# A four-layer transformer: norm weights on x instead of the matrices, and head probabilities turned by DMA in all layers

## The chip, the cores and the metric

The kernel runs on one core of a Trainium2 chip. A core has TensorE (PE), VectorE (DVE), ScalarE (ACT), GpSimd (POOL) and SyncE (SP), each with its own queue of instructions that it works off in order, and 16 DMA engines. The metric is the time of one execution in microseconds; lower is better.

## The reference, cut to what matters

256 tokens of width 1024 go through four layers. Each layer is attention, a gated feed-forward part (hidden width 2816) and a gate on a side input, each behind a norm:

```python
def rmsnorm(x, g, eps=NORM_EPS):
    xf = x.astype(jnp.float32)
    y = xf * lax.rsqrt(jnp.mean(xf * xf, axis=-1, keepdims=True) + eps)
    return (y * g.astype(jnp.float32)).astype(x.dtype)
...
    for i in range(DEPTH):                       # DEPTH = 2, twice
        hn = rmsnorm(h, norm_mix[i])
        ...                                      # mix = attention(hn): another kind in each of the four layers
        h = h + mix
        h = h + swiglu(rmsnorm(h, norm_ffn[i]), ffn_w_gate[i], ffn_w_up[i], ffn_w_down[i])
        gate = jax.nn.sigmoid(rmsnorm(h, norm_ple[i]) @ ple_w_gate[i])
        h = h + gate * (p[i] @ ple_w_proj[i])
```

The four attentions are differential attention (`L_DA`: `a[0] - lam * a[1]`, then a norm over each head), neighbourhood attention (`L_NA`), stick-breaking attention (`L_SB`) and forgetting attention (`L_FX`: queries and keys have norms of their own, `rms_norm(split_heads(...), ...)`, and its queries see `attn_norm_g`, its keys and values `shared_norm_g`). All are float32.

## The kernel before

**Tiling.** The weights stream through a ring of six slots (`raw`, `RING`) in units of 128 x 1024 floats. A layer is a row of 108 units, numbered `s`: 24 for queries, keys and values (`U_QKV`), 8 for the attention's output (`U_WO`), 4 + 60 for gate and up and down (`U_GU0`, `U_FFN`), 4 for the last down and the side input, 8 for the gate (`U_GATE`). The 16 heads are worked in four groups `j` (0 to 3), each with four query/key units and two value units, so a group takes six units.

**Float32 by three products.** TensorE multiplies in a rounded format. Each factor is split: ACT copies `raw` to the rounded `whi` and DVE takes the rest, `wlo = raw - whi` (`split`); PE then adds three products of each pair (`three`, lines 1618 to 1620; 1729 to 1731 where x stands on the streaming side), 12 products with 512 columns for most units. x is split in the same way into `xhi` and `xlo`. Norm weights multiply the matrix in this step: for units behind a norm, `split` gets a column of `gain` as scale, in two pieces of 512 (`unit_parts`). The norm's root factor is applied behind the products.

**The turned x.** At each norm PE turns h in four quarters (`turn_x`, quarter `q` = half of the columns, half of the rows), into two PSUM banks `tb` in turns; for each quarter ACT writes `xhi` (line 861) and DVE `xlo` (1160), each in one instruction of 128 x 512. At a layer's end DVE computes h quarter by quarter (`gated_side`, 1184 and 1186), with `xlo` of quarters 0 and 1 between; PE turns quarters 2 and 3 in `first_pair`, between its 12 products for the first tile and those for the second.

**Attention.** What runs at which unit is a table for each engine (`PE_STEPS`, `ACT_STEPS`, `DVE_STEPS`): row `r` of group `j` runs at unit `s = 6 j + r + 4`; a name with `+` behind the unit's own work. Per group: scores on PE, bias and maximum on DVE, exponentials on ACT (`exp0`, `exp1` for the two tiles of 128 queries), normalization on DVE (`post0`, `post1`), then the probabilities `z` are turned and multiplied with the values (`pvt`; `pv0`, `pv1`, `turno` in the first layer). `V_WAITS` says at which row the product with the values runs in groups that do not use the table's own.

**Two ways of turning.** PE turns `z` with `turn` (line 1779) in batches of four blocks (`turnp0`, `turnp1`), and ACT (960, 963) and DVE (1389) copy the batches out of PSUM. With `by_dma` true (groups 0 to 2 of the second and third layers), DVE splits each probability into its two 16-bit halves (`split_p`, 1255), SP issues a DMA transpose (554), and ACT joins the halves again (`join`, 946).

**The fourth layer.** ACT squares the raw queries and keys, DVE sums the squares (1340), POOL takes the root (704, 706), DVE scales (1363), and only then can PE turn them (`turnqk0`, `turnqk1`) and compute scores.

## Time and profile before

| | us |
|---|---|
| median of 3 runs (1313.96 to 1315.85) | 1314.66 |
| the profiled execution | 1316.3 |
| its span, first to last instruction | 1314.5 |
| PE busy | 1300.8 |
| DVE busy | 958.0 |
| ACT busy | 847.8 |
| POOL busy | 130.7 |

Read it so: PE has something in flight for 99% of the span, and is TensorE at its upper clock nearly throughout. Matmuls overlap, so the time that one costs is the distance to the next one's start, and a stall is a longer distance. Rows of a timeline carry their own start times, so who is late by how much can be read off.

### The profile page before, as it was taken

The page shows a single profiled execution, that of the slowest core. Times are in us where ns is not written, and L with a number is a line of the kernel's source. Part 1 is how long each engine was busy: PE and PEld are TensorE (multiplying, and loading weights), DVE is VectorE, ACT ScalarE, POOL GpSimd, SP SyncE. Part 2 cuts the span into 40 slices and gives each one's busy share as a digit, 9 for nine tenths or more (in the row PEclk, how much of TensorE's full clock was granted, in tenths as well). Part 3 has the DMA queues.
Part 4 walks back from the last instruction along what each step waited for, and adds up shares of the span by engine and source line. Part 5 has one row for each costly group of instructions (what it writes and reads, how often), then busy time and mean ns, then how long its engine had stood idle before and what let it go on. Part 6 is the DMA issues. An engine that isn't in the chain of part 4 may idle for free.

```text
span 1314.5 us, 20037 instructions
## 1 busy us (share of the span) xinstructions
PE 1300.8 (99%) x6642; PEld 1084.5 (83%) x6642; DVE 958.0 (73%) x1661; ACT 847.8 (64%) x1459; POOL 130.7 (10%) x179
## 2 busy tenths in 40 slices
PE   8999999999999999999999999999999999999998
PEld 7988888888887788888888888888887778888887
DVE  6887687666898766666699976666677887666664
ACT  7666666656777666665676666666578766666654
POOL 6031234410000000000010000000002210000000
PEclk9999999999999999999999999999999999999999
DMA  9444788876496566667647656666655535676671
GB/s 336 145 156 137 221 243 245 239 226 200 167 222 174 162 198 207 207 207 211 210 149 196 181 174 195 210 210 206 212 161 185 178 127 168 199 209 210 209 226 48
DMA packets 205056, 255.28 MB, mean 194 GB/s; under 512 B 72962, under 2 KB 163249, under 8 KB 204992
## 3 DMA queue, kind: packets, MB, share of 16 engines
q1 hardware_dynamic: 201984, 245.42, 60.8%
q0 software_dynamic: 2832, 8.49, 2.8%
q8 instruction: 37, 0.61, 0.2%
q10 hardware_dynamic: 176, 0.54, 0.1%
q14 instruction: 27, 0.22, 0.1%
HBM read 238.33 MB, written 1.13 MB: 182 GB/s over the span
## 4 chain that ended last, share of the span: by engine, by line
PE 92%; DVE 5%; ACT 1%; DMA 1%; issue 1%; SPq 1%; POOL 0%; DVEq 0%; ACTq 0%
PE acc L1618 14%; PE acc L1620 14%; PE acc L1619 14%; PE sc L1620 12%; PE sc L1619 12%; PE sc L1618 12%; PE turn L1779 3%; PE acc L1729 2%; PE acc L1730 2%; PE acc L1731 2%; PE turn L1881 1%; DVE wlo L1140 1%; DMA raw<-in_da_w_qkv 1%; PE sc L1832 1%; DVE z L1299 1%
## 5 line engine op out<-in xcount | busy, mean ns | idle before, releaser
L830 ACT ACTIVATE whi<-raw,aT_gain 128x512 fp32r<-128x512 f32 (+2 forms) x612 | 403.6, 719 | 79.1 <-PE sc L1620 53.4
L1140 DVE SCALAR_TENSOR_TENSOR wlo<-raw,aT_gain,whi 128x512 fp32r<-128x512 f32 (+2 forms) x612 | 431.0, 759 | 28.7 <-ACT whi L830 24.6
L1618 PE MATMUL sc<-whi,xhi 128*128 128x512 f32 x640 | 249.3, 390 | 0.0
L1620 PE MATMUL sc<-whi,xlo 128*128 128x512 f32 x640 | 249.0, 389 | 0.0
L1619 PE MATMUL sc<-wlo,xhi 128*128 128x512 f32 x640 | 249.0, 389 | 0.0
L1618 PE MATMUL acc<-whi,xhi 128*128 128x512 f32 x432 | 173.3, 401 | 1.8 <-DVE wlo L1140 1.4
L1620 PE MATMUL acc<-whi,xlo 128*128 128x512 f32 x432 | 168.5, 390 | 0.0
L1619 PE MATMUL acc<-wlo,xhi 128*128 128x512 f32 x432 | 168.5, 390 | 0.0
L830 ACT ACTIVATE whi<-raw 128x1024 fp32r<-128x1024 f32 x120 | 125.8, 1055 | 63.5 <-PE acc L1620 56.9
L1138 DVE TENSOR_TENSOR wlo<-raw,whi 128x1024 fp32r<-128x1024 f32 x120 | 145.5, 1244 | 0.0
L1619 PEld LDWEIGHTS sc<-wlo,xhi 128*128 128x128 f32 x640 | 120.1, 188 | 25.0
L1618 PEld LDWEIGHTS sc<-whi,xhi 128*128 128x128 f32 x640 | 120.1, 188 | 24.9
L1620 PEld LDWEIGHTS sc<-whi,xlo 128*128 128x128 f32 x640 | 120.1, 188 | 24.7
L1415 DVE SCALAR_TENSOR_TENSOR aT_gain<-sc,rstd,aT_gain 128x256 f32<-128x256 f32 x80 | 38.7, 484 | 114.7 <-ACT aT_gain L979 114.7
L979 ACT ACTIVATE aT_gain<-sc,rstd 128x256 f32<-128x256 f32 x80 | 38.0, 475 | 127.0 <-PE sc L1620 127.0
L1618 PE MATMUL acc<-whi,split_qg 128*128 128x512 f32 x288 | 112.4, 390 | 0.0
L1620 PE MATMUL acc<-whi,split_qg 128*128 128x512 f32 x288 | 112.1, 389 | 0.0
L1619 PE MATMUL acc<-wlo,split_qg 128*128 128x512 f32 x288 | 112.1, 389 | 0.0
L1618 PEld LDWEIGHTS acc<-whi,xhi 128*128 128x128 f32 x432 | 81.3, 188 | 19.0 <-DVE wlo L1140 1.9
L1620 PEld LDWEIGHTS acc<-whi,xlo 128*128 128x128 f32 x432 | 81.1, 188 | 17.4
L673 POOL TENSOR_SCALAR rstd<-ss 128x2 f32<-128x2 f32 x12 | 2.7, 222 | 917.3 <-ACT spare L853 917.3
L1619 PEld LDWEIGHTS acc<-wlo,xhi 128*128 128x128 f32 x432 | 81.4, 189 | 15.0
(213 smaller groups left out, 2069.6 us busy)
## 6 DMA issues: line engine op xcount, KB each, us to landing
raw<-in_ffn_w_gu SPq DMA_DIRECT2D x176, 256.0 KB
raw<-in_qk SPq DMA_DIRECT2D x62, 512.0 KB
raw<-in_ffn_w_gate SPq DMA_DIRECT2D x88, 256.0 KB
raw<-in_ffn_w_up SPq DMA_DIRECT2D x88, 256.0 KB
raw<-in_ffn_w_down SPq DMA_DIRECT2D x44, 512.0 KB
raw<-in_ffn_w_d SPq DMA_DIRECT2D x44, 512.0 KB
raw<-in_ple_w_gate SPq DMA_DIRECT2D x32, 512.0 KB
raw<-in_da_w_qkv SPq DMA_DIRECT2D x8, 512.0 KB
```

Source lines behind the costliest of these rows:

```text
L830: ins = act.activation(whi[:, u % RING, c0:c1], raw[:, u % RING, c0:c1], ACT.Copy, scale=scale)
L979: act.activation(aT[:, 0, t * 256:t * 256 + 256], bank[:, 0:256], ACT.Sigmoid, scale=rs(L, 1, t))\
L1138: ins = dve.tensor_tensor(lo, w, hi.bitcast(F32), ALU.subtract)
L1140: ins = dve.scalar_tensor_tensor(out=lo, in0=w, scalar=gain[:, g:g + 1], in1=hi.bitcast(F32), op0=ALU.mult, op1=ALU.subtract)
L1415: dve.scalar_tensor_tensor(out=sg, in0=banks[t][:, 256:512], scalar=rs(L, 1, t), in1=sg, op0=ALU.mult, op1=ALU.mult).then_inc(gmid, 1)
L1618: pe.matmul(dst, xh, wh, start=first, stop=False)
L1619: pe.matmul(dst, xh, wl, start=False, stop=False)
L1620: return pe.matmul(dst, xl, wh, start=False, stop=last)
L1729: pe.matmul(dst, wh, xh, start=first and k == 0 and c == 0, stop=False)
L1730: pe.matmul(dst, wl, xh, start=False, stop=False)
L1731: ins = pe.matmul(dst, wh, xl, start=False, stop=last and k == 1 and c == 1)
L1779: ins = pe.transpose(tb[e % 2][0:cols, n * rows:(n + 1) * rows], src, ident[0:rows, 0:rows])
```

## The change

1. Norm weights are taken off the matrices. A weight unit behind a norm is now split in one piece of 1024 without scale; the weight columns go onto x where it is split. Since a norm weight belongs to one block of 128 columns of h, each quarter of x is now written in four pieces of 128 x 128 by ACT and four by DVE. DVE begins when ACT's four are done (`turn_hi` counts once a quarter). PE waits for single pieces (`wait_x`) in `first_pair` and at the gate. The fourth layer's first norm keeps its weights on the matrix (two norms share that x), but its x too is written in pieces. The 256 x 1024 input x in the beginning is split in pieces of one block as well.
2. `by_dma` is true for head groups 0 to 2 of all four layers. In the first layer there are two maps to turn and not four (`p_maps`), since the difference is taken ahead.
3. The products with the values move to later rows: in the fourth layer from row 8 to 10, in the first layer for group 1 from rows 6, 7 and 8 to 8, 9 and 10. `join0` and `join1` are added to ACT's tables of both layers.

```diff
@@ tables @@
-    L_DA: [["evacqk"], ["turnqk"], [], ["exp0"], ["exp1"], ["turnp0"], ["pv0", "turnp1"], ["pv1*"], ["turno*"]],
+    L_DA: [["evacqk"], ["turnqk"], [], ["exp0"], ["exp1"], ["turnp0"], ["pv0", "turnp1"], ["pv1*", "join0"],
+           ["turno*", "join1"]],
...
-    L_FX: [["evacqk"], [], ["turnqk0", "turnqk1+"], [], ["exp0", "exp1+"], ["turnp0"], ["turnp1"], ["pvt*"]],
+    L_FX: [["evacqk"], [], ["turnqk0", "turnqk1+"], [], ["exp0", "exp1+"], ["turnp0"], ["turnp1"], ["pvt*"], ["join0"], ["join1"]],
...
-V_WAITS = {L_DA: {"pv0": 8, "pv1": 9, "turno": 10}, L_NA: {"pvt": 9}, L_SB: {"pvt": 10}, L_FX: {"pvt": 8}}
+V_WAITS = {L_DA: {"pv0": 8, "pv1": 9, "turno": 10}, L_NA: {"pvt": 9}, L_SB: {"pvt": 10}, L_FX: {"pvt": 10}}
...
-            if j % 2 == 0 or (L == L_FX or joined(L)) and j < HG - 1:
+            if j < HG - 1:
...
-    return L in (L_NA, L_SB,) and j < HG - 1
+    return L in (L_DA, L_NA, L_SB, L_FX,) and j < HG - 1
@@ ACT, turn_x @@
                     act.wait_ge(turned, e + 1)
-                    act.activation(xhi[:, 4 * hf:4 * hf + 4, t * P:(t + 1) * P],
-                                   tb[e % 2][:, :].rearrange("p (k c) -> p k c", k=4), ACT.Copy).then_inc(turn_hi, 1)
+                    for k in range(4):
+                        g = x_gain(L, n, 4 * hf + k)
+                        ins = act.activation(xhi[:, 4 * hf + k, t * P:(t + 1) * P], tb[e % 2][:, k * P:(k + 1) * P],
+                                             ACT.Copy, scale=1.0 if g is None else gain[:, g:g + 1])
+                    ins.then_inc(turn_hi, 1)
@@ DVE, turn_x @@
+                    dve.wait_ge(turn_hi, SPLIT[("x", L, n, q)])
+                    for k in range(4):
+                        g, at = x_gain(L, n, 4 * hf + k), (slice(None), 4 * hf + k, slice(t * P, (t + 1) * P))
+                        src = tb[e % 2][:, k * P:(k + 1) * P]
...
+                        ins.then_inc(x_lo if k < 3 else turn_out[e % 2], 1)
@@ DVE, after_exp, first layer @@
                     ins.then_inc(a_ready, 1)
+                    if by_dma(L, j):
+                        dve.wait_ge(a_ready, 2 * j + t + 1)
+                        split_p(L, j, t)
                     return
@@ PE, first_pair @@
                         for k in range(2):
+                            wait_x(pe, L, n, t, 2 * b + k)
```

**Order on ACT, fourth layer.** Around the exponentials of group 1 (`z,sums<-z,mx`; `whi` is a weight unit in pieces). Before:

```order
L830 ACTIVATE whi<-raw,aT_gain 128x512 [waits unit_done,weights_in5]
L830 ACTIVATE whi<-raw,aT_gain 128x512
L974 ACTIVATE ohi<-turn 128x512 [waits turned]
L936 ACTIVATE z,sums<-z,mx 128x128 [waits mx_ready]
L936 ACTIVATE z,sums<-z,mx 128x128 x3
L830 ACTIVATE whi<-raw,aT_gain 128x256 [waits unit_done,weights_in0]
L830 ACTIVATE whi<-raw,aT_gain 128x256 x3
L936 ACTIVATE z,sums<-z,mx 128x256 [waits mx_ready]
L936 ACTIVATE z,sums<-z,mx 128x256 x3
L960 ACTIVATE aT_gain<-turn 128x4x128 [waits turned]
L830 ACTIVATE whi<-raw,aT_gain 128x256 [waits unit_done,weights_in1]
```

Now:

```order
L959 ACTIVATE bias<-aT_gain 128x4x128 [waits p_turned0]
L959 ACTIVATE bias<-aT_gain 128x4x128
L841 ACTIVATE whi<-raw,aT_gain 128x512 [waits unit_done,weights_in5]
L841 ACTIVATE whi<-raw,aT_gain 128x512
L949 ACTIVATE z,sums<-z,mx 128x128 [waits mx_ready]
L949 ACTIVATE z,sums<-z,mx 128x128 x3
L959 ACTIVATE bias<-aT_gain 128x1024 [waits p_turned1]
L959 ACTIVATE bias<-aT_gain 128x1024
L841 ACTIVATE whi<-raw,aT_gain 128x256 [waits unit_done,weights_in0]
L841 ACTIVATE whi<-raw,aT_gain 128x256 x3
L949 ACTIVATE z,sums<-z,mx 128x256 [waits mx_ready]
L949 ACTIVATE z,sums<-z,mx 128x256 x3
```

The join of group 0's second tile (`bias<-aT_gain`, 128x1024 twice) stands between the two tiles' exponentials, and the copy of the head output (`ohi`) has moved behind them.

**Order on DVE, fourth layer.** From the normalization of group 0's second tile (`z<-z,rsum`) to the scaling of group 1's queries and keys (`qkv<-acc,r_h`). Before:

```order
L1297 RECIPROCAL rsum<-sums 128x4 [waits e_ready]
L1299 TENSOR_TENSOR z<-z,rsum 128x1024 [waits dve_link]
L1340 TENSOR_REDUCE ss_h<-nab 128x8 [waits sq_ready] x2
L1140 SCALAR_TENSOR_TENSOR wlo<-raw,aT_gain,whi 128x256 [waits hi_done]
L1140 SCALAR_TENSOR_TENSOR wlo<-raw,aT_gain,whi 128x256 x3
L1363 TENSOR_TENSOR qkv<-acc,r_h 128x512 [waits rh_ready] x2
L1389 COPY aT_gain<-turn 128x512 [waits turned]
```

Now:

```order
L1321 RECIPROCAL rsum<-sums 128x4 [waits e_ready]
L1323 TENSOR_TENSOR z<-z,rsum 128x1024 [waits dve_link]
L1276 COPY bias<-z 128x1024 [waits p_ready]
L1276 COPY bias<-z 128x1024
L1364 TENSOR_REDUCE ss_h<-nab 128x8 [waits sq_ready] x2
L1156 SCALAR_TENSOR_TENSOR wlo<-raw,aT_gain,whi 128x256 [waits hi_done]
L1156 SCALAR_TENSOR_TENSOR wlo<-raw,aT_gain,whi 128x256 x3
L1387 TENSOR_TENSOR qkv<-acc,r_h 128x512 [waits rh_ready] x2
```

Two copies (`bias<-z`) stand ahead of the sum of squares (`ss_h<-nab`), and the copy of turned probabilities (`aT_gain<-turn`) is gone.

**Order on DVE, end of the first layer.** Quarters 1 to 3 of h and of `xlo`. Before:

```order
L1184 TENSOR_TENSOR aT_gain<-aT_gain,z 128x512 [waits proj_out,gate_sig]
L1186 TENSOR_TENSOR h<-h,aT_gain 128x512 [waits gated]
L1160 TENSOR_TENSOR xlo<-turn,xhi 128x4x128 [waits turn_hi]
L1184 TENSOR_TENSOR aT_gain<-aT_gain,z 128x512 [waits proj_out,gate_sig]
L1186 TENSOR_TENSOR h<-h,aT_gain 128x512 [waits gated]
L1160 TENSOR_TENSOR xlo<-turn,xhi 128x4x128 [waits turn_hi]
L1184 TENSOR_TENSOR aT_gain<-aT_gain,z 128x512 [waits proj_out,gate_sig]
L1186 TENSOR_TENSOR h<-h,aT_gain 128x512 [waits gated]
```

Now:

```order
L1205 TENSOR_TENSOR aT_gain<-aT_gain,z 128x512 [waits proj_out,gate_sig]
L1207 TENSOR_TENSOR h<-h,aT_gain 128x512 [waits gated]
L1187 SCALAR_TENSOR_TENSOR xlo<-turn,aT_gain,xhi 128x128 [waits turn_hi]
L1187 SCALAR_TENSOR_TENSOR xlo<-turn,aT_gain,xhi 128x128 x3
L1205 TENSOR_TENSOR aT_gain<-aT_gain,z 128x512 [waits proj_out,gate_sig]
L1207 TENSOR_TENSOR h<-h,aT_gain 128x512 [waits gated]
L1187 SCALAR_TENSOR_TENSOR xlo<-turn,aT_gain,xhi 128x128 [waits turn_hi]
L1187 SCALAR_TENSOR_TENSOR xlo<-turn,aT_gain,xhi 128x128 x3
L1205 TENSOR_TENSOR aT_gain<-aT_gain,z 128x512 [waits proj_out,gate_sig]
L1207 TENSOR_TENSOR h<-h,aT_gain 128x512 [waits gated]
```

The order is the same; each `xlo` is four instructions.

## Rows read from the trace of the kernel before

**Rows 1.** The page's first table: busy time, share of the span and instructions of each engine.

```profile
PE 1300.8 (99%) x6642; PEld 1084.5 (83%) x6642; DVE 958.0 (73%) x1661; ACT 847.8 (64%) x1459; POOL 130.7 (10%) x179
```

**Rows 2.** Instructions by line and shape, whole run: out<-in, count | busy us, mean ns | idle before.

```profile
L1140 DVE SCALAR_TENSOR_TENSOR wlo<-raw,aT_gain,whi 128x512 fp32r<-128x512 f32 x508 | 354.3, 754 | 20.9 <-ACT whi L830 16.8
L830 ACT ACTIVATE whi<-raw,aT_gain 128x512 fp32r<-128x512 f32 x508 | 331.7, 713 | 67.1 <-PE sc L1620 53.4 <-PE acc L1620 11.4 <-PE acc L1731 0.9
L1138 DVE TENSOR_TENSOR wlo<-raw,whi 128x1024 fp32r<-128x1024 f32 x120 | 145.5, 1244 | 0.0
L830 ACT ACTIVATE whi<-raw 128x1024 fp32r<-128x1024 f32 x120 | 125.8, 1055 | 63.5 <-PE acc L1620 56.9 <-PE sc L1620 6.6
L1160 DVE TENSOR_TENSOR xlo<-turn,xhi 128x512 fp32r<-128x512 f32 x44 | 29.0, 686 | 21.6 <-ACT xhi L861 21.5
L946 ACT ACTIVATE bias<-aT_gain 128x1024 uint16<-128x1024 uint16 x18 | 23.2, 1354 | 1.4 <-DMA aT_gain<-bias 1.4
L861 ACT ACTIVATE xhi<-turn 128x512 fp32r<-128x512 f32 x44 | 24.7, 598 | 28.8 <-PE turn L1779 28.8
L1779 PE MATMUL turn<-ident,z 128*128 128x128 f32 x108 | 15.5, 276 | 1.1 <-DVE z L1293 0.6 <-DVE z L1299 0.5
L1255 DVE COPY bias<-z 128x1024 uint16<-128x1024 uint16 x18 | 11.6, 688 | 0.2
L1140 DVE SCALAR_TENSOR_TENSOR wlo<-raw,aT_gain,whi 128x256 fp32r<-128x256 f32 x64 | 26.6, 479 | 3.4 <-ACT whi L830 3.4
L1429 DVE COPY aT_gain<-aT_gain 128x512 uint16<-128x512 uint16 x72 | 27.9, 430 | 1.2
L916 ACT ACTIVATE fin_gain<-turn,aT_gain 128x256 f32<-128x256 f32 x8 | 3.8, 472 | 9.9 <-PE turn L1779 9.9
```

**Rows 3.** Waits of PE, timeline of PE, and a window (busy, granted clock, DMA share, GB/s), second layer.

```profile
PE sc L1832 <- DVE split_qg L1349: 3.7, 2, 2.0
...
395.44 0.39 PE L1832 MATMUL sc<-qkT 64*128 64x256 f32 x2 [2.03 <-DVE split_qg L1349]
...
397.00:400.00 3.00, 3.00 (x17) 0.50 0.85 300
```

**Rows 4.** Timeline of DVE at the start: start us, us, line, operation [idle before <-releaser].

```profile
13.05 1.41 DVE L1140 SCALAR_TENSOR_TENSOR wlo<-raw,aT_gain,whi 128x512 fp32r<-128x512 f32 x2 [1.33 <-ACT whi L830]
```

**Rows 5.** Timelines of ACT, DVE and PE, end of the first layer.

```profile
333.43 0.60 ACT L861 ACTIVATE xhi<-turn 128x512 fp32r<-128x512 f32 x1 [1.11 <-PE turn L1779]
...
337.31 0.69 DVE L1186 TENSOR_TENSOR h<-h,aT_gain 128x512 f32<-128x512 f32 x1
...
337.81 0.60 PE L1779 MATMUL turn<-ident,h 128*128 128x128 f32 x4
```

**Rows 6.** Timelines of DVE and PE, first layer, head group 2.

```profile
68.66 1.42 DVE L1353 TENSOR_TENSOR split_qg<-qkv,qkT 128x256 fp32r<-128x256 f32 x4
...
72.00 0.39 PE L1832 MATMUL sc<-qkT 64*128 64x256 f32 x2
```

**Rows 7.** Timelines of PE, DVE and POOL, fourth layer, head groups 0 and 1.

```profile
1018.98 1.04 PE L1779 MATMUL turn<-ident,z 128*128 128x128 f32 x8
1019.77 0.48 PE L1618 MATMUL acc<-whi,xhi 128*128 128x512 f32 x1
...
1022.60 0.60 PE L1779 MATMUL turn<-ident,qkv 128*128 128x128 f32 x4
...
1018.52 1.27 DVE L1340 TENSOR_REDUCE ss_h<-nab 128x8 f32<-128x512 f32 x2
...
1023.45 0.69 DVE L1363 TENSOR_TENSOR qkv<-acc,r_h 128x512 f32<-128x512 f32 x1 [1.40 <-POOL r_h L706]
...
1019.66 1.66 POOL L706 TENSOR_TENSOR r_h<-r_h,powm 128x8 f32<-128x8 f32 x1
```

**Rows 8.** Timelines of ACT and PE, fourth layer, head groups 1 and 2.

```profile
1035.56 0.49 ACT L936 ACTIVATE z<-z,mx 128x256 f32<-128x256 f32 x1
...
1045.95 0.49 PE L1779 MATMUL turn<-ident,qkv 128*128 128x128 f32 x3
```

More of the change, by code:

```diff
@@ L288, in unit_parts, with x_gain @@
 def unit_parts(L, s):
[L290 removed]
+    if s < U_WO and L == L_FX:
         b = s % GROUP_UNITS
[L292 removed]
         if b >= QK_UNITS:
[L294 removed]
+            at = GAIN_SHARED + V_UNITS * 2 * (s // GROUP_UNITS % 2) + 2 * (b - QK_UNITS)
             return [(512 * k, 512 * k + 512, at + k) for k in range(2)]
[L296 to L309 removed]
+        return [(512 * k + 256 * x, 512 * k + 256 * x + 256, g + 2 * b + k)
+                for k in range(2) for x, g in enumerate((GAIN_MIX[L], GAIN_SHARED))]
+    if L == L_DA and U_WO <= s < U_GU0:
+        return [(0, 1024, GAIN_SUB)]
+    return [(0, 1024, None)]
+def x_gain(L, n, kb):
+    if (L, n) == (L_FX, 0):
+        return None
+    return (GAIN_MIX, GAIN_FFN, GAIN_PLE)[n][L] + kb
 def build(nc, a, out):
@@ L453, in wait_out, with p_maps, wait_x @@
             eng.wait_ge(turn_out[e % 2], e // 2 + 1)
+        def p_maps(L):
+            return 2 if L == L_DA else 4
         def p_source(L, j, t):
-            return bias[:, t, j, :].bitcast(U16)[:, 0:8 * keys(L, t)]
+            return bias[:, t, j, :].bitcast(U16)[:, 0:2 * p_maps(L) * keys(L, t)]
         def p_target(L, t):
-            return aT[:, t, :].bitcast(U16)[:, 0:8 * keys(L, t)]
+            return aT[:, t, :].bitcast(U16)[:, 0:2 * p_maps(L) * keys(L, t)]
         def p_halves(tile, L, t, h):
-            return tile.bitcast(U16).rearrange("p (x c h) -> p x c h", c=S, h=2)[:, :, 0:keys(L, t), h]
+            return tile.bitcast(U16).rearrange("p (x c h) -> p x c h", c=S, h=2)[:, 0:p_maps(L), 0:keys(L, t), h]
+        def wait_x(eng, L, n, q, k):
+            if k == 3:
+                wait_out(eng, EV[("x", L, n, q)])
+            else:
+                eng.wait_ge(x_lo, 3 * (X_TURN[("x", L, n, q)] - 1) + k + 1)
         def scores_wait(eng, L, j, t):
@@ L833, in split_part @@
             def split_part(u, k):
-                g = GAIN_MIX[0] + 2 * u + k
                 act.wait_ge(part_in[2 * u + k], 16)
-                act.activation(whi[:, u, 512 * k:512 * k + 512], raw[:, u, 512 * k:512 * k + 512], ACT.Copy,
-                               scale=gain[:, g:g + 1]).then_inc(hi_done, 1)
+                act.activation(whi[:, u, 512 * k:512 * k + 512], raw[:, u, 512 * k:512 * k + 512], ACT.Copy)\
+                    .then_inc(hi_done, 1)
             def split_ahead(L, s):
@@ L985, in split_x @@
                 act.wait_ge(x_t_in[n], 16)
-                act.activation(xhi[:, k0:k1, :], x_block(k0, k1), ACT.Copy).then_inc(x_t_hi, 1)
+                for kb in range(k0, k1):
+                    g = x_gain(0, 0, kb)
+                    ins = act.activation(xhi[:, kb, :], x_block(kb, kb + 1)[:, 0, :], ACT.Copy, scale=gain[:, g:g + 1])
+                ins.then_inc(x_t_hi, 1)
             for u in range(2):
@@ L1438, in split_x @@
                 dve.wait_ge(x_t_hi, n + 1)
-                dve.tensor_tensor(xlo[:, k0:k1, :], x_block(k0, k1), xhi[:, k0:k1, :].bitcast(F32), ALU.subtract)\
-                    .then_inc(x_t_lo, 1)
+                for kb in range(k0, k1):
+                    g = x_gain(0, 0, kb)
+                    ins = dve.scalar_tensor_tensor(out=xlo[:, kb, :], in0=x_block(kb, kb + 1)[:, 0, :],
+                                                   scalar=gain[:, g:g + 1], in1=xhi[:, kb, :].bitcast(F32),
+                                                   op0=ALU.mult, op1=ALU.subtract)
+                ins.then_inc(x_t_lo, 1)
             for u in range(2):
@@ L1855, in attention @@
                     use(e)
-                    wait_out(pe, EV[("p", L, j, t, 0)])
+                    if by_dma(L, j):
+                        pe.wait_ge(p_joined, P_TURN[(L, j, t)])
+                    else:
+                        wait_out(pe, EV[("p", L, j, t, 0)])
+                    p_t = bias[:, t, j, :] if by_dma(L, j) else aT[:, t, :]
                     for kt in range(T):
@@ L2002, in _ @@
                 for kb in range(KB - 2):
-                    if kb in (0, 4):
-                        for q in range(2):
-                            wait_out(pe, EV[("x", L, 2, q + (2 if kb else 0))])
+                    for t in range(T):
+                        wait_x(pe, L, 2, 2 * (kb // 4) + t, kb % 4)
                     wide_unit(L, U_GATE + kb, kb, xhi, xlo, kb == 0, False, G_GATE)
```

42 lines of the change are left out of this document (12 added, 30 removed).

## The prediction

> **What bounds the kernel now.** I read the busy table first: PE is busy for 1300.8 of 1314.5 us [rows 1]. The timeline of PE then shows it dense: a 512-column product starts 0.227 us after the last one, and nearly all of PE's order is such products. So the program goes by the number of PE's instructions, and by the few places where PE waits. The largest waits are both in the second layer, for the low halves of queries and keys (3.7 us in two, of 2.0 and 1.7), and the first of them has a tail: behind the gap the granted clock is 0.50, which is 1.2 instead of 2.4 GHz, for some 3.4 us [rows 3]. At half the speed that costs half of it, 1.7 us. DVE (958 us) and ACT (848 us) have slack on the average, but in the attention stages they run in chains that end just before PE needs their result. There the change adds work to both. The views that matter are therefore the timelines of DVE and ACT at those places, against the moment when PE arrives.
>
> **What it removes.** PE's batches of probabilities: six of four blocks in the first layer, three of four and three of eight in the fourth. A batch of eight starts at 1018.98 and the next product at 1019.77 [rows 7]: 0.79 us; a batch of four takes 0.36 in the same view. That is 9 x 0.36 + 3 x 0.79 = 5.6 us, 60 of the 108 instructions of that row in [rows 2]. PE also waits 1.1 us before some of them [rows 2], and 0.4 before 1024.79 for DVE's copy of the last one. Together **-7.1 us** if nothing else becomes late.
>
> **Weight units without a scale.** Two pieces of 512 cost DVE 1.41 us together [rows 4] and ACT about 1.33 (two of 713 ns, overlapping); one of 1024 costs 1.24 and 1.06 [rows 2], some 0.1 less where the next one overlaps. The units are split 4 to 8 us ahead of PE almost everywhere, so 0.2 to 0.3 us per unit is worth nothing by itself: feed-forward, which is two thirds of the program, does not change. It is worth something where the chain is tight. At the start PE waits 1.6 us for unit 2, whose ACT pieces and DVE pieces [rows 4] follow each other: 0.28 + 0.17 = **-0.45**. In the second layer three splits on DVE stand in the chain ahead of the 2.0 us wait and one ahead of the 1.7 us wait: 4 x 0.19 = **-0.8**. The first gap is then 1.5 us, below the second one of today (1.7), behind which the clock stayed up; so I also take away its tail: **-1.7**.
>
> **x in pieces.** An ACT piece of 128 columns with a scale: 256 columns take 472 ns, and a column costs 0.9 ns or a little less (1055 for 1024, 598 for 512), so 0.36 us; neighbours overlap by about 0.1, as the two pieces of 754 ns in [rows 4] do, so 0.27 from start to start, and four take 1.17 instead of 0.60 [rows 2]. DVE: 754 ns for 512, 479 for 256 [rows 2], so 0.34 for 128, 0.26 apart, four take 1.13 instead of 0.69. At the end of the first layer h's last quarter is done at 337.31 + 0.69 = 338.00, and PE wants to turn it at 338.25, right behind quarter 2 [rows 5]. The new chain from quarter 0's turning: ACT 333.43 to 334.60; DVE's four to 335.77; h of quarter 2 to 337.1; DVE's four of quarter 1 to 338.15; h of quarter 3 to 339.46. PE stalls 1.2 us, and 0.1 more ahead of `first_pair`, since the first piece comes at 335.05 against 334.96. PE cannot pass this: the turning stands in its queue ahead of the second tile's products. The same rows recur at the end of the second layer; at the third, without scales, the pieces are cheaper and I get 0.4. At the four feed-forward norms the last quarter of h comes just in time, 0.1 each. At the gates there are over 3 us of room. Sum 2 x 1.3 + 0.4 + 0.4 = **+3.4**. Below: no stall, if pieces overlap more than 256-column ones do. Above: +5, with pieces 0.1 dearer each.
>
> The Trainium skill ("ScalarE: Activation LUTs", the section What ACT_TABLE_LOAD costs) gives 186 ns + 0.833 ns a column for an ACTIVATE, 93 ns more for a scale read from a column, and an overlap of 93 ns between two. By it four pieces are 1.27 us and not 1.17, and the sum would be about 0.5 us higher. Where the trace has the same thing it agrees: 512 columns with a scale are 705 ns by that rule and 713 in [rows 2]. Pieces of 128 columns are in no row.
>
> **First layer, probabilities by DMA.** DVE gets two 16-bit copies per tile. Copies of 512 take 0.43 each [rows 2], so 0.78 a tile. The DMA and the join (1354 ns for a half of 1024 [rows 2], 0.75 here) have two to three units of 3 us each and fit. The low halves of group 2's keys end at 68.66 + 1.42 = 70.09 and PE starts its scores at 72.00 [rows 6], 1.9 us later. Now DVE ends 2 x 0.8 later, less 0.6 of cheaper splits and 0.4 for a head output moved away: 70.7. But PE arrives earlier: two batches and a wait less (1.1), and two products with the values moved behind (1.9), so at 69.0. Stall **+1.7**. For groups 1 and 3 the two meet; 0.1.
>
> **Fourth layer, group 1.** The chain is DVE's sum of squares (start 1018.52), POOL's root, DVE's scaling, PE's turning. POOL's first root ends at 1019.66 + 1.66 = 1021.32, that is 2.8 us after the sum started; the second scaling waits for POOL until 1023.45, 4.9 after it [rows 7]. DVE now has 0.8 and 1.35 us of copies ahead of it (688 ns for a half of the larger tile [rows 2]). The first scaling ends at 1024.2. PE, without three batches' worth, arrives at 1021.4 and not 1022.60: stall 2.8; the second half 0.35. The product with the values of group 0, which filled the time between the two scores, now comes later, and PE waits 0.95 for DVE to free the bank.
>
> **Group 2.** ACT's second exponentials started at 1035.56 [rows 8] and now stand behind a join of 2.6 us (two of 1354 ns [rows 2], overlapping). With DVE's copies and a wait inherited from before, POOL's chain starts 5 us later; the first scaling ends at 1049.5. PE turned at 1045.95 [rows 8]; it would arrive at 1047.2. Stalls 2.3, 0.35, and 0.85 ahead of the scores, where a join is in ACT's way again. **Group 3:** the same sum gives 0.1, 0.4 and 0.6. Together 2.8 + 0.35 + 0.95 + 2.3 + 0.35 + 0.85 + 0.1 + 0.4 + 0.6 = **+8.7**. From below: if DVE's delay had cover, PE would lose nothing here; from above, every copy and join on the path is (0.8 + 1.35 + 2.6) x 3, 14 us. I take the step-by-step sum. Two of these stalls are longer than the gap that drew the clock down; one of the two, I assume, does so again: **+1.7**.
>
> SP's queue: a DMA transpose holds it for some 2 us ahead of later weight loads, which are issued over 10 us before ACT takes them. That costs nothing. The work of the last group, the feed-forward part and the end are untouched.
>
> **Sum**, against the profiled execution: -7.1 - 0.45 - 0.8 - 1.7 + 3.4 + 1.7 + 0.1 + 8.7 + 1.7 = +5.6 us. The profiled execution took 1316.3, 1.6 over the median of 1314.66; I add the difference to the median: **1320.2 us**.
>
> **Rivals.**
> 1. *The waits are covered and only the removal is left* (not slower). It needs DVE and ACT to be early by more than I read: the scalings of the fourth layer in time for PE's arrival, and h's last quarter before 338.25. For it: in both engines the page shows a quarter or more idle. Against: each of these chains has under 2 us of room today. -7.1 - 0.45 - 0.8 - 1.7 is -10; with some 3 us of stalls left, 1307.5. The point is 10 us of new stalls: under it the change gains, and under 7.4 by more than 0.2%.
> 2. *The stalls come to about half.* PE's waits overlap: a stall in one place gives DVE and ACT time to catch up at the next. +15.6 becomes +8 to +12: 1312.7 to 1316.7, within what can be told from no change (0.2% is 2.6 us, about what a measurement of this kernel tells).
> 3. *The fourth layer goes from bad to worse*: each long stall draws the clock down (+1.7 each for three more), and the joins wait for their transposes behind weight loads; 1326 to 1330.
>
> That lighter weight splitting shows nowhere in the feed-forward part, where it has most of its instructions, is already in the sum; the terms of the norm weights alone are -2.95 against +3.4, so that half of the change would not be told from none.
>
> **Chances.** Forecast 0.53 (1317.5 to 1325), rival 1 0.15, rival 2 0.22, rival 3 0.10. Rival 2's cases lie mostly within 2.6 us of 1314.66, a few below. Faster by over 0.2%: 0.18; within: 0.22; slower: 0.60. The range takes in the forecast, most of rival 2 and the edge of rivals 1 and 3: 1309 to 1326.
>
> **What the profile after would show.** PE's waits in the fourth layer for `qkv` (scaling) and POOL's root, 2 to 3 us each at groups 1 and 2: right. ACT's second exponentials of group 1 behind the joins: right. At the ends of the first and second layers PE waiting about 1.2 us for h's last quarter: right. The 2.0 us wait of the second layer shortened, with no 0.50 clock behind it: right. A wait of 1.7 us ahead of group 2's scores in the first layer. The forecast is wrong if PE's new waits come to under 10 us in all, and its reasons are wrong if they are there but elsewhere, such as behind `p_joined` or a weight unit.

## The result, and the profile after

The changed kernel takes **1327.47 us** (median of four executions, 1326.17 to 1328.46); the kernel before, timed beside it, 1315.09 (1313.96 to 1315.85). The ratio is 1.0093, 95% interval [1.0081, 1.0106]: slower by 12.4 us, or 0.9%. The forecast was 1320.2, in a range of 1309 to 1326. The direction was right and the size was off by more than half of the effect. The profiled execution took 1327.97 us (span 1326.2).

The busy line answers to [rows 1]. PE has 60 instructions fewer and DVE and ACT have 13 and 30 us less to do, and yet the span is 11.7 us longer:

```profile
PE 1299.0 (98%) x6582; PEld 1079.9 (81%) x6582; DVE 944.7 (71%) x1572; ACT 818.0 (62%) x1361; POOL 131.7 (10%) x179
```

PE's waits after (engine, what waits, for whom, us in total, times, longest) answer to the first line of [rows 3]:

```profile
PE turn L1805 <- DVE qkv L1387: 7.2, 3, 3.1
PE sc L1858 <- DVE split_qg L1377: 4.1, 2, 2.5
PE sc L1858 <- DVE split_qg L1373: 2.9, 2, 1.5
PE turn L1805 <- DVE h L1207: 2.4, 3, 1.0
...
PE turn L1851 <- DVE spare L1497: 0.8, 1, 0.8
PE sc L1851 <- issue: 0.7, 1, 0.7
```

The first line is the scaled queries and keys of the fourth layer, groups 1 to 3. The second is new: the low halves in the first layer, groups 2 and 3. The third is the two waits of the second layer, 3.7 us before. The fourth is h's last quarter at the ends of layers. No line names `p_joined` or, beyond the start, a weight unit.

Four windows of the same execution (busy, granted clock, DMA share, GB/s) show PE at 0.50, which is 1.2 of 2.4 GHz, two in the first layer and two in the fourth; [rows 3] had one, in the second layer, and there is none there now:

```profile
70.00:72.00 2.00, 2.00 (x11) 0.50 0.77 219
94.00:96.00 2.00, 2.00 (x13) 0.50 0.64 211
1029.00:1031.00 2.00, 2.00 (x7) 0.50 0.86 254
1080.00:1083.00 3.00, 3.00 (x9) 0.50 0.23 65
```

Each stretch is some 3.4 us long and loses 1.7. All four belong to a wait of PE, and only the first begins when PE is at work again: the granted clock is 0.79 from 93.00 to 93.40 and 0.50 from 1028.50 to 1028.85, and PE does nothing in either window. In PE's timeline (start, us, operation, [idle before <- releaser]) the waits are:

```profile
67.97 0.39 PE L1858 MATMUL sc<-qkT 64*128 64x256 f32 x2 [1.62 <-DVE split_qg L1377]
...
93.42 0.58 PE L1858 MATMUL sc<-qkT 64*128 64x256 f32 x2 [2.53 <-DVE split_qg L1377]
...
1028.88 1.09 PE L1805 MATMUL turn<-ident,qkv 128*128 128x128 f32 x4 [3.10 <-DVE qkv L1387]
...
1054.12 0.63 PE L1805 MATMUL turn<-ident,qkv 128*128 128x128 f32 x4 [2.54 <-DVE qkv L1387]
...
1077.92 0.63 PE L1805 MATMUL turn<-ident,qkv 128*128 128x128 f32 x4 [1.51 <-DVE qkv L1387]
...
1079.92 0.80 PE L1646 MATMUL acc<-whi,ohi 128*128 128x512 f32 x1 [0.67 <-DVE qkv L1387]
```

I measure a wait as the distance between two starts less the usual one; so counted, these are 1.78, 2.69, 3.26, 2.71, 1.67 and 0.84 us. The last two stand 2 us apart, and the fourth stretch begins in the second of them, before 1079.92. To see where the time goes I cut each trace where PE turns h's first quarter for a norm. The attention segment of a layer, in us (the four feed-forward segments are 186.4 to 186.5 in every kernel; the last column leaves out a stretch at 1.2 GHz that every trace has behind PE's last product):

| kernel (profiled execution) | first | second | third | fourth | us lost at 1.2 GHz |
|---|---|---|---|---|---|
| before | 121.49 | 114.91 | 107.17 | 119.51 | 1.7 |
| after | 123.85 | 113.97 | 109.14 | 126.94 | 6.8 |
| weights on x only | 119.47 | 114.03 | 109.14 | 120.33 | 0 |
| weights left out, x whole | 119.53 | 112.68 | 107.18 | 119.48 | 0 |
| DMA turning only | 127.58 | 114.92 | 107.18 | 126.53 | 10.2 |
| weights on x, DMA first layer | 122.50 | 113.97 | 109.13 | 120.00 | 1.7 |
| weights on x, DMA fourth layer | 120.06 | 113.97 | 109.16 | 126.48 | 1.7 |

After against before: +2.4, -0.9, +2.0, +7.4, and 0.9 in the other segments together.

### The profile page after: what moved, and what is told of

Same layout as the page of the kernel before. It is cut to its first block, busy times and chain, and to the rows that moved or that the text cites. A ratio compares the mean times of both kernels' runs of the same rounds, so it can differ in the third digit from the quotient of the medians.

```text
span 1326.2 us, 19766 instructions
## 1 busy us (share of the span) xinstructions
PE 1299.0 (98%) x6582; PEld 1079.9 (81%) x6582; DVE 944.7 (71%) x1572; ACT 818.0 (62%) x1361; POOL 131.7 (10%) x179
## 4 chain that ended last, share of the span: by engine, by line
PE 88%; DVE 8%; ACT 2%; POOL 1%; issue 1%; DMA 0%; SPq 0%; DVEq 0%; ACTq 0%; POOLq 0%
PE acc L1646 14%; PE acc L1647 13%; PE acc L1648 13%; PE sc L1646 12%; PE sc L1647 11%; PE sc L1648 11%; PE turn L1805 2%; PE acc L1755 2%; PE acc L1757 2%; PE acc L1756 2%; PE turn L1911 1%; DVE wlo L1154 1%; DVE bias L1276 1%; PE sc L1858 1%; DVE wlo L1156 1%
## 5 line engine op out<-in xcount | busy, mean ns | idle before, releaser
L841 ACT ACTIVATE whi<-raw 128x1024 fp32r<-128x1024 f32 x398 | 413.3, 1057 | 159.5 <-PE acc L1648 90.6
L1154 DVE TENSOR_TENSOR wlo<-raw,whi 128x1024 fp32r<-128x1024 f32 x398 | 482.7, 1253 | 18.8 <-ACT whi L841 14.7
L1598 DVE TENSOR_TENSOR split_qg<-z,split_qg 128x512 fp32r<-128x512 f32 x36 | 24.9, 692 | 88.8 <-ACT split_qg L1092 88.8
L1755 PE MATMUL acc<-xhi,whi 128*128 128x256 f32 x288 | 84.2, 292 | 0.0
```

The source lines that it names most:

```text
L841: ins = act.activation(whi[:, u % RING, c0:c1], raw[:, u % RING, c0:c1], ACT.Copy, scale=scale)
L1154: ins = dve.tensor_tensor(lo, w, hi.bitcast(F32), ALU.subtract)
L1598: dve.tensor_tensor(glo, joined_g.rearrange("p (k s) -> p k s", k=2), ghi.bitcast(F32), ALU.subtract).then_inc(g_lo, 1)
L1755: pe.matmul(dst, wh, xh, start=first and k == 0 and c == 0, stop=False)
```

## The experiments

### One half of the change at a time

The theory: the DMA turning in the first and fourth layers loses, through waits on DVE and the clock behind them, and the norm weights come out near even. The rival A: the four pieces of x, which stand in every layer, are the larger part. Four kernels undo one part each (where the DMA turning goes, the rows of the products with the values and the joins in ACT's table go back with it). The kernels were timed in several sessions, on different chips, each with the kernel before beside them; its median moved between 1314.37 and 1315.63, so a difference of medians across sessions is good to about 1 us.

```
e1:  return L in (L_NA, L_SB,) and j < HG - 1          # by_dma as before, norm weights on x
e2:  return L in (L_DA, L_NA, L_SB, L_FX,) and ...     # by_dma as after, unit_parts and x as before
e3:  return L in (L_DA, L_NA, L_SB,) and j < HG - 1
e4:  return L in (L_NA, L_SB, L_FX,) and j < HG - 1
```

> The norm weights on x as in the change, but the probabilities of the first and fourth layers turned by PE as before. Theory (the loss comes from the DMA turning in the first and fourth layers and from the clock drops behind its waits, the norm weights come out even): 1314 to 1317 us, PE's waits in the fourth layer as before, no clock drop except none or one in the second layer. Rival A (the norm weights on x are the larger part of the loss, because their four pieces delay DVE and ACT everywhere): 1321 us or more.

> The DMA turning in all four layers, the norm weights on the matrices as before. Theory: +2.4 us from the first layer and +7.4 from the fourth (the shifts between the two traces there), so 1323 to 1327 us, and three or four stretches at 1.2 GHz behind waits of 1.7 us and more, plus the one of the second layer. Rival A (norm weights are the larger part): 1319 or less.

> The change without the DMA turning of the fourth layer (that of the first layer stays). Theory: the shift of 2.4 us that the trace has at the end of the first layer's attention, on top of the norm weights: 1317 to 1320 us, with the 2.7 us wait ahead of group 3's scores and two stretches at 1.2 GHz in the first layer. Rival A: 1324 or more, since the norm weights and not the fourth layer make the loss. Rival B (only the fourth layer loses, the first gains its six batches): 1315 or less.

> The change without the DMA turning of the first layer (that of the fourth stays). Theory: 7.4 us of the fourth layer on top of the norm weights: 1322 to 1325 us, waits of 3.3, 2.7 and 1.7 us ahead of the turning of queries and keys there. Rival A: 1325 or more. Rival B (only the fourth layer loses): 1327, no better than the whole change.

Measured, against a before of 1315.63 on the same chip: e1 1317.40 (ratio 1.0023 [1.0013, 1.0033]), e2 1327.99 (1.0089 [1.0073, 1.0105]), e3 1320.03 (1.0042 [1.0028, 1.0056]), e4 1323.90 (1.0068 [1.0054, 1.0082]). So the first layer's DMA turning costs 2.6 us, the fourth's 6.5, and rival A falls: alone the weights on x cost 1.8 us by the medians and 3.0 by the ratio, and e1 lies 0.4 above its band. Rival B falls too: the first layer loses. The three costs sum to 10.9 us, where the whole change costs 12.4; and e2, without the weights on x, costs 12.4 by itself, so the parts add only roughly. e2 landed 1.0 above its band: five executions of it spread from 1323.61 to 1329.49, and their mean granted clocks order them, 0.997 at the low end and 0.992 at the high one. I take this to mean that the same program has more or fewer stretches at half the clock from one execution to the next. e3 shows this within a trace: its first wait is 1.78 us as in the changed kernel, and nothing follows; behind its second, of 2.69, the clock falls:

```profile
69.00:73.00 4.00, 4.00 (x36) 1.00 0.70 217
93.00:95.00 2.00, 2.00 (x11) 0.50 0.53 176
```

### What the pieces of x cost

```
e5, on the kernel before:
-        return [(512 * k, 512 * k + 512, GAIN_MIX[L] + 2 * b + k) for k in range(2)]
...
+    return [(0, 1024, None)]                 # and the same for the feed-forward and gate units
```

> The kernel before with the norm weights left out where the change puts them on x: the weight units are split unscaled in pieces of 1024, x stays one instruction per quarter, and the weights multiply nothing (the output is another). Theory (units without a scale save 0.5 us at the start, 0.8 in the second layer and at times its clock tail of 1.7; the pieces of x are what costs): 1312 to 1315 us, 3 to 4 under the run with the norm weights on x, and no wait of 1.2 us at the ends of the first and second layers. Rival (the pieces of x are free and the units save nothing either): 1315 to 1318, like the run with the norm weights on x.

Measured 1312.45 (0.9978 [0.9969, 0.9987]), in the band. Against e1 that is 5.0 us for the pieces (by the medians and by the profiled spans), and the segments place it: 1.35 in the second layer, 1.96 in the third, 0.85 in the fourth, the rest 0.1 at each feed-forward norm and gate. It is more than the 3 to 4 expected. In the timings of the changed kernel's pieces nothing is off from what I worked out (first their group over the whole run, then DVE's timeline at the end of the first layer):

```profile
L873 ACT ACTIVATE xhi<-turn,aT_gain 128x128 fp32r<-128x128 f32 x160 | 44.6, 397 | 25.8 <-PE turn L1805 25.6
```

```profile
338.91 0.69 DVE L1207 TENSOR_TENSOR h<-h,aT_gain 128x512 f32<-128x512 f32 x1
339.52 1.12 DVE L1187 SCALAR_TENSOR_TENSOR xlo<-turn,aT_gain,xhi 128x128 fp32r<-128x128 f32 x4
...
341.27 0.69 DVE L1207 TENSOR_TENSOR h<-h,aT_gain 128x512 f32<-128x512 f32 x1
```

The four take 1.12 us on DVE and 1.14 to 1.15 on ACT. By the rule that the prediction quoted from the Trainium skill ("ScalarE: Activation LUTs", What ACT_TABLE_LOAD costs) ACT's would be 1.27; the measurement decides. So what the pieces cost beyond my sum does not come from the length of a piece. And h's last quarter comes 1.2 us after PE wants it, at both layer ends, as forecast. What I had left out is the third layer's `rs_across` (the wait of 0.8 on `spare` above, 0.2 in the kernel before): DVE comes to it late at the start of that layer. In e11 below, where the third layer's x is whole again, that wait is back at 0.2.

### Is it the clock?

PE's waits were filled with products of the identity, whose output the next operation overwrites:

```
+            def fill(dst, n):
+                for _ in range(n):
+                    pe.matmul(dst, ident[:, :], ident[:, :], start=True, stop=True)
...
+                    if name == "scores0" and L == L_DA and j in (2, 3):
+                        pe.wait_ge(z_ready, ATT[(L, j, t)] - 1)
+                        fill(sc[:, 0, 0:P], FILL[(L, j)])
...
                         use(e)
+                        if t == 0 and (L, j) in FILL:
+                            fill(tb[e % 2][:, 0:P], FILL[(L, j)])
```

> The change, with products of the identity on PE (12 and 20 in the first layer, ahead of the scores of groups 2 and 3; 24, 19 and 10 in the fourth, ahead of the turning of queries and keys) in place of most of the waiting; about 0.12 us each, written where the next operation overwrites them. Theory (what the waits cost beyond their length is the clock that falls to 1.2 GHz behind them): the same waits with PE busy in them, no stretch at 0.50 behind, 3 to 6 us less, 1321.5 to 1324.5. Rival C (the clock falls for another reason, or costs nothing): 1326.5 to 1330.

This one went wrong by my own sum: a product took 0.237 us and not 0.12 (24 records of 12 products in 2.84 us), so the fillings overran the waits by some 8 us in all. Measured 1330.77 (1.0114 [1.0098, 1.0129]), 3.3 more than the change, with no stretch at 0.50 before PE's end. It adds less than it overruns by, but decides nothing. So again with shorter ones:

> The change with shorter fillings of PE's waits: 7 and 11 products of the identity in the first layer, 13, 11 and 6 in the fourth, at 0.236 us each as the long fillings showed (1.7, 2.6, 3.1, 2.6 and 1.4 us, just under the waits). Theory (each wait of 1.7 us and more costs its length and, in most executions, the clock behind it): no stretch at 0.50, no wait longer than before, 3 to 6 us under the change: 1321.5 to 1324.5. Rival C (the clock costs nothing in the end, since PE would wait later instead): 1326.5 to 1329.

Measured 1324.95 (1.0076 [1.0062, 1.0089]), half a microsecond above the band and 2.5 below the change. No stretch at 0.50 is left before PE's end (three windows, and a row of PE's timeline):

```profile
68.00:72.00 4.00, 3.95 (x38) 1.00 0.76 222
90.00:96.00 6.00, 5.89 (x45) 1.00 0.80 231
1026.00:1031.00 5.00, 4.75 (x31) 1.00 0.84 265
```

```profile
1035.15 1.13 PE L1862 MATMUL sc<-fin_gain 64*128 64x256 f32 x8 [1.05 <-DVE mx L1258]
```

The last line tells why the four stretches, which lose 6.8 us by themselves, were worth only 3.2 of the profiled time. The first layer's segment got 2.5 shorter, the fourth's only 0.8: there PE, back at speed, waits 1.05 us for DVE ahead of group 1's second scores, where it did not wait in the changed kernel. So a stretch at 1.2 GHz costs less than its 1.7 us where PE is about to wait again; the fourth layer is the one place that shows it. The time landed between theory and rival C: by this run the clock's share of the 12.4 us is 2.5.

### Are DVE's copies and ACT's joins in the chain?

```
e7, fourth layer: copies of the second tile between the next group's scalings; join behind its exponentials
                     for t in range(T):
+                        if t and j:
+                            planes_p(L, j - 1, 1)
                         dve.wait_ge(rh_ready, 2 * j + t + 1)
...
+                    names = [x for x in names if x != "join1"] + (["join1+"] if r == 10 else [])
e8, first layer: copies behind the next group's low halves
-    ... ["post0"], ["post1"], ["pv0", "turnp1"], ["pv1*"],
+    ... ["post0"], ["post1"], ["pv0", "turnp1"], ["pv1*", "planes1"],
```

> The change, with two things moved in the fourth layer: DVE's copies of the second tile's probabilities go between the two scalings of the next group, where DVE waits for POOL's root, and the join of the second tile goes behind the next group's second exponentials on ACT (the product with the values of groups 0 and 1 one unit later for it). Theory (copies and joins in the chain DVE, POOL, DVE make the fourth layer's waits): the waits ahead of the turning fall from 3.3, 2.7 and 1.7 us by 1.3 each and the second by another 1.3, and the clock drops with them: 1319 to 1323 us. Rival D (PE waits since it arrives earlier, or for DMA): 1326 or more.

> The change, with DVE's copies of the second tile's probabilities in the first layer moved behind the low halves of the next group's queries and keys (and the join behind that unit's weight split). Theory: the waits ahead of the scores of groups 2 and 3 fall from 1.8 and 2.7 us by 0.8 each, 1.6 us less and up to two clock drops less: 1323 to 1326 us. Rival D (they come from PE's earlier arrival alone, and DVE's copies have no part in it): 1327 or more.

Measured: e7 1322.84 (1.0054 [1.0041, 1.0068]), e8 1324.45 (1.0068 [1.0054, 1.0082]), both in their bands. In e7 two of the fourth layer's three long waits are gone and one is 1.8 (idle time as the view has it, 3.1 before), and what is left has moved, partly to the product with the values; in e8 the pair of the first layer is down from 4.1 to 2.6 (PE's waits in e7, then in e8):

```profile
PE turn L1815 <- DVE qkv L1397: 1.8, 1, 1.8
...
PE turn L1921 <- ACT bias L967: 1.4, 2, 1.1
PE sc L1861 <- DVE mx L1266: 1.1, 1, 1.1
```

```profile
PE sc L1869 <- DVE split_qg L1388: 2.6, 2, 1.8
```

> The change with both moves together: DVE's copies and the joins of the second tile out of the chain in the first layer and in the fourth. Theory (the two are independent, 4.6 and 3.0 us): 1319 to 1321 us, over the kernel before by 4 or 5, since PE still waits for 1.0 and 2.0 us in the first layer, 1.9 and 1.2 in the fourth, and 1.2 at two layer ends. Rival (the first layer's shift and the fourth's clock drops are one and the same loss, so that they don't add): 1322 or more.

Measured 1319.05 (1.0031 [1.0019, 1.0043]): 8.4 under the change, where the two apart gave 4.6 and 3.0. They add, within what medians of two sessions tell.

### Can the rest be mended?

```
e11:
-    if (L, n) == (L_FX, 0):
+    if L >= L_SB and n == 0:                 # x whole, weights on the third layer's matrices
         return None
...
+                        pool.tensor_tensor(aT[:, t, c], aT[:, t, c], z[:, t, c], ALU.mult).then_inc(gated_p, 1)
```

> Norm weights on x with PE turning the first and fourth layers' probabilities, and two edits at the ends of layers: the first norms of the third and fourth layers keep x in one piece per quarter (the third's weights stay on its matrices), and POOL multiplies the gate of h's last two quarters. Theory (the pieces cost by delaying h's last quarter): the waits of 1.2 and 0.5 us at the ends of the second and third layers go, that of 0.9 in the third with them, the one at the end of the first falls to about 0.5: 1314 to 1315.5 us, no slower than before. Rival (POOL's multiplication is slower than DVE's and holds h up instead): 1317 or more.

> The last kernel and the first layer's probabilities turned by DMA, with the copies and the join of the second tile moved out of the chain as before. Theory: 2.6 us for the DMA turning, less 3.0 for the move, so 1313 to 1315 us, as fast as the kernel before or up to 2 us faster. Rival (the waits of 1.0 and 2.0 us ahead of the scores keep their clock drops, which eat the six batches): 1316 to 1318.

Both missed: e11 took 1316.27 (1.0011 [1.0002, 1.0020]), e13 1317.62 (1.0020 [1.0011, 1.0029]). In e11 the third layer's segment is 107.87, as expected, but the end of the first layer still waits 1.1 us and the ends of the second and third 0.7: POOL's multiplication is no quicker a way. e11 lies between its theory and its rival. e13 lies in its rival's band; its executions spread from 1316.16 to 1319.19, the longer ones with mean clocks of 0.998 and 0.999. That clock drops make the difference is not shown: the profiled execution (1316.23) has the wait of 2.0 us ahead of group 3's scores and no stretch at 0.50 behind it.

### What the kernel before was

The executions of the kernel before have two lengths. In one session of 27 executions 17 took 1313.85 to 1314.69 at a mean clock of 1.000, and 10 took 1315.44 to 1316.17 at 0.998 or 0.999. The profiled one, 1316.3, is of the second kind.

```
e16, on the kernel before; e17 is e14 with the same lines; e14 has norm weights on x in the first norm alone, e15 in the first norms of two layers
+                    if name == "scores0" and L == L_NA and j == 2:
+                        pe.wait_ge(z_ready, ATT[(L, j, t)] - 1)
+                        for _ in range(8):
+                            pe.matmul(sc[:, 0, 0:P], ident[:, :], ident[:, :], start=True, stop=True)
```

> The kernel before, with eight products of the identity (1.9 us) in its wait of 2.2 us ahead of the third group's scores of the second layer. Theory (the kernel before runs in two lengths, 1314.2 with a mean clock of 1.000 and 1315.7 with 0.999 or less, and this wait is what tells them apart): nearly all executions at 1314 to 1314.5, none with a stretch at 0.50 there. Rival (the two lengths have another cause): both lengths as before, median 1314.4 to 1315.6.

> The kernel before, with the norm weights on x only in the first norm of the first layer, where x comes turned from memory and no chain stands behind its pieces. Theory (the weights on x pay only where their pieces have cover: the trace with all norm weights on x has 2.0 us less in that segment and nothing or a loss in the others): 1312 to 1313.5 us, faster than before by 1.5 to 2. Rival (the 2.0 us belong to the later norms' lighter units, and the first norm gives the 0.45 us of its wait): 1314 to 1315.

> The kernel before with the norm weights on x in the first norms of the first and second layers. Theory: the pieces at the end of the first layer cost 1.2 us and the lighter units of the second layer save 0.8 and the clock tail that the kernel before has in some of its executions (1.7, half of them), so together with the first norm 1311.5 to 1313.5 us. Rival (the pieces outweigh it): 1314 or more.

> The kernel before with the norm weights on x in the first norm alone, and eight products of the identity in PE's wait ahead of the second layer's third group. Theory (the first norm is worth up to 1.3 us, part of it hidden by the varying arrival at the start; the filling takes away the slower of the two lengths): 1312.9 to 1314, all executions within 1.5 us, faster than before by 0.5 to 1.5. Rival (the first norm is worth nothing): 1314.0 to 1314.6, as with the filling alone.

e16: all eleven executions between 1314.02 and 1314.56, one length, and the window that held the stretch of [rows 3] is at full clock:

```profile
392.00:400.00 8.00, 7.76 (x73) 1.00 0.99 241
```

That settles it: the clock drop of [rows 3] is in some of the executions only, 10 of the 27 here, and is worth 1.5 us. e14 (1314.53, 0.9997 [0.9988, 1.0006]) and e15 (1313.72, 0.9995 [0.9986, 1.0004]) can't be told from the kernel before. Both are over their bands, e14 by 1.0 us and in its rival's, e15 by 0.2. e14's executions run from 1312.94 to 1316.03, and the three longest have clocks of 0.998 and 0.999. e17 is 1313.31 (0.9989 [0.9980, 0.9998]), in its band. It is the only kernel of the study that computes the whole and is faster than the one before: by 1.4 us by the ratio, with an interval from 0.3 to 2.6, from one norm and a filled wait. How much of it is the norm is not shown; e16, with the filling alone, was timed in another session and is 0.9 above it.

### A root of 2.78 us

Group 3 of the fourth layer was given 0.1 us and waits 1.67. Its first root on POOL takes 2.78 us where all others take 1.64 to 2.04; so also in the other kernels whose copies stand in the chain of that layer (e2, e4, e6, e8, e9). DVE begins a subtraction of 1024 columns 0.04 us after the root. Two kernels change that subtraction alone:

> The change, with DVE's subtraction of the unscaled weight units at the fourth layer's fourth group in two halves of 512 (0.66 us) in place of one of 1024 (1.22 us). Theory (POOL's root of group 3 waits for the one instruction that DVE has begun, to its end): the root takes 1.66 + some 0.55 = 2.2 us and PE's wait there falls by 0.5, from 1.67 to 1.1 or 1.2. Rival E (it waits for something else, or as long as DVE works at all): 2.78 as before.

> The change, with the same units in DVE's other form (multiplied by 1 and subtracted in one instruction of 1024 columns, some 1.27 us). Theory (it is the form: beside the scaled form POOL's roots took 1.66 in all kernels, though always with pieces of 256): 1.66 us, PE's wait there 0.5 to 0.6. Rival F (any long instruction with both inputs in SBUF holds the root): 2.8 us or more.

The lines of POOL and DVE in the changed kernel, in e18, in e19, and in e7, where the root is short:

```profile
1074.27 2.78 POOL L717 TENSOR_TENSOR r_h<-r_h,powm 128x8 f32<-128x8 f32 x1
...
1074.31 1.22 DVE L1154 TENSOR_TENSOR wlo<-raw,whi 128x1024 fp32r<-128x1024 f32 x1
```

```profile
1073.61 2.85 POOL L717 TENSOR_TENSOR r_h<-r_h,powm 128x8 f32<-128x8 f32 x1
...
1073.65 1.28 DVE L1155 TENSOR_TENSOR wlo<-raw,whi 128x512 fp32r<-128x512 f32 x2
```

```profile
1073.00 2.78 POOL L717 TENSOR_TENSOR r_h<-r_h,powm 128x8 f32<-128x8 f32 x1
...
1073.04 1.22 DVE L1154 SCALAR_TENSOR_TENSOR wlo<-raw,whi 128x1024 fp32r<-128x1024 f32 x1
```

```profile
1071.80 1.66 POOL L725 TENSOR_TENSOR r_h<-r_h,powm 128x8 f32<-128x8 f32 x1
...
1071.85 1.24 DVE L1162 TENSOR_TENSOR wlo<-raw,whi 128x1024 fp32r<-128x1024 f32 x1
```

Both of my theories fell, and the rivals come nearest: halving the instruction does not shorten the root (2.85), and the form is not it (2.78). (Each of the two kernels ran once, in 1327.54 and 1326.70 us, within the spread of the change; only the rows count here.) What the three have in common is the end: the root ends 1.52 or 1.53 us after DVE's subtraction, or the pair of them, has ended, as if it had begun only then. The Trainium skill ("SBUF — State Buffer", section Who interferes with whom) says that a DVE instruction with two inputs in SBUF contends with a GpSimd instruction that reads SBUF, and that the order of issue decides who blocks; its section SBUF: two separate sides adds that whoever starts first has the shared ports for the whole instruction. The three traces agree with a blocked POOL, though their rows show POOL starting first, and in e18 POOL did not get in between two DVE instructions of 0.68 us, which overlap by 0.08. In the kernel before a copy out of PSUM stands between, the same subtraction begins 0.64 us after the root (1064.66 against 1064.02), and the root takes 1.66. What decides who is first is open: in e7 and in the kernel with both moves the starts are 0.05 and 0.04 us apart in the same order, and the root is 1.66. By the wait the effect is worth 1.1 us; no run here isolated it in the time.

## Why the prediction was wrong, point by point

**What bounds the kernel, and how:** right. PE's waits on DVE's chains decide, and they are where I put them except one.

**The base: wrong by about 1.5 us.** The profiled execution had a clock drop that the median of 1314.66, at the edge of the shorter of the two lengths, does not hold. I worked out a difference against that execution, with -1.7 for its tail, and added it to the median. From profile to profile my sum says 1316.3 + 5.6 = 1321.9, against 1327.97.

**Removal and weight units:** the second layer's waits are 1.62 each (2.2 and 1.8 before), no clock drop follows, right. At the start the traces of e1 and before differ by 2.0 us where I said 0.45, but e14's median shows that the executions don't as a rule; PE reaches the first scores at 25.4 to 26.8 us in the traces of kernels with the lighter first units, and at 26.7 to 27.2 in the others.

**x in pieces:** the mechanism and 1.2 us at each of two layer ends right; the term +3.4 measured 5.0 (e1 against e5). Missing were 0.7 in the third layer's segment, with the wait on `spare`, 0.4 in the fourth's, and 0.5 at the feed-forward norms and gates, which cost 0.9 and not 0.4.

**First layer: the step that failed.** Group 2 was stepped through: +1.7 forecast, 1.78 measured. For group 3 I wrote that the two meet, 0.1, without the same steps. It waits 2.69. First DVE and PE before, then DVE after:

```profile
89.39 1.43 DVE L1353 TENSOR_TENSOR split_qg<-qkv,qkT 128x256 fp32r<-128x256 f32 x4 [0.83 <-ACT qkT L901]
...
92.47 0.38 PE L1832 MATMUL sc<-qkT 64*128 64x256 f32 x2
```

```profile
87.63 0.76 DVE L1276 COPY bias<-z 128x512 uint16<-128x512 uint16 x2
...
91.90 1.42 DVE L1377 TENSOR_TENSOR split_qg<-qkv,qkT 128x256 fp32r<-128x256 f32 x4
```

DVE ends the low halves at 93.32, 2.5 us later than before (90.82), with two pairs of copies ahead of it (1.05 us at 83.22, 0.76 at 87.63) and, ahead of the second pair, the split of a head output (`olo`, 0.68) that ran earlier before; PE, without two batches and a product, arrives at 90.7 instead of 92.5. PE is 1.7 us earlier and DVE 2.5 later, against a slack of 1.65 before: that makes 2.6 of the 2.69. The copies are a part of it only: with the second pair moved away (e8) it falls by 0.7. The two times before were in the trace when I wrote the prediction; I had read DVE's up to group 2 only. And I gave this layer no clock drop, though I forecast a wait of 1.7 in it, against 2.0 for the one in [rows 3] that had drawn one; it has two, 3.4 us. Together the two are 6.0 us over the forecast. My sum for the segment was -1.4, it is +2.4; that is 3.8 us of the miss, since PE also came to the first scores 1.5 us earlier than before and not 0.45, and the rest of the segment is shorter than my sum by 1.3 us, which no run here resolves.

**Fourth layer:** the sum was right, the parts less so. Forecast for the segment +6.5, measured +7.4. The three turnings wait 3.26, 2.71 and 1.67 (forecast 2.8, 2.3, 0.1). Group 3's is too low by the long root of 1.1 us and a part that I didn't resolve. The two clock drops together cost 0.8 by e9's segment, less than the 1.7 that I added for one, since PE waits again behind them.

**Rivals.** The first two are out. The third, fourth layer from bad to worse and a clock drop for each long stall, gave 1326 to 1330, which holds the result; its clock part is what happened, but half of it in the first layer, and the joins' waits for their transposes come to 1.4 us of ACT in all, as in the kernel before. That the result lies in its range owes something to luck: the first layer's group 3 is not in it.

Summed over the profiled executions: 3.8 first layer, 0.9 fourth, 0.7 third, 0.5 feed-forward and gates, 0.3 second; but for rounding that is the 6.1 between 1321.9 and 1327.97.

## What to carry to other kernels

Where a change makes PE arrive earlier and its supplier later at several places of the same pattern, step through each of them: the group that is waved through as "the two meet" is the one that costs. A wait of PE near 2 us has a price of its own behind it, the clock, in some executions and not in others; look whether the profiled execution had it, and whether its time lies at the edge of the timed ones, before adding a difference to the median. And taking work from the bounding engine by DMA loads the others: here a removed batch (0.36 to 0.79 us of PE) put copies of up to 1.3 us and joins of up to 2.6 us a tile into chains with under 2 us of room.

## What the runs showed of the hardware

- The granted clock of PE was 0.50 (1.2 GHz) for 3.4 us (1.7 lost) behind a wait of 1.78 us in the changed kernel, and not behind a wait of the same length in e3; behind 2.69 us in both; behind 3.26 us in the changed kernel, and not behind 2.71 there. The length of the wait alone does not decide. Behind the waits of 1.62 us in the second layer it fell in no trace. It differs between executions of one kernel: 10 of 27 of the kernel before are 1.5 us longer, with mean clocks of 0.998 or 0.999 in place of 1.000.
- With the waits filled by products of the identity, no trace has a stretch at 0.50 before PE's end (e6, e9, e16, e17), and the kernel before goes from two lengths to one (e16: eleven executions at 1314.02 to 1314.56).
- POOL's root of 128x8 took 2.78 to 2.85 us instead of 1.66 beside DVE's subtractions with both inputs in SBUF that began 0.04 us after it, and ended 1.52 or 1.53 us after them; in e7 and with both moves it took 1.66 beside the same subtraction.
